# Gated delta rule: the next group's preparation placed step by step in the scan, the last state update left out, and block transfers on two queues

## The reference, cut to what matters

```python
decay = jnp.exp(jnp.where(lower, gc[..., :, None] - gc[..., None, :], -jnp.inf))
a = jnp.where(strict, jnp.einsum('bhncd,bhnsd->bhncs', kb, kc) * decay, 0.0)
t_inv = lax.linalg.triangular_solve(eye + a, jnp.broadcast_to(eye, a.shape),
                                    left_side=True, lower=True, unit_diagonal=True)
...
qk = jnp.einsum('bhncd,bhnsd->bhncs', qc, kc) * decay
...
def step(s, xs):
    qk_i, qd_i, kd_i, u_i, w_i, gl_i = xs
    v_new = u_i - jnp.einsum('bhcd,bhde->bhce', w_i, s)
    o = jnp.einsum('bhcd,bhde->bhce', qd_i, s) + jnp.einsum('bhcs,bhse->bhce', qk_i, v_new)
    s = s * gl_i[..., None, None] + jnp.einsum('bhcd,bhce->bhde', kd_i, v_new)
    return s, o
```

## Time and profile before

| | us |
|---|---|
| median of 3 runs | 3377.32 (3372.14 to 3378.64) |
| the profiled execution | 3375.33 |
| its span, first to last instruction | 3373.5 |
| delta rule's eight groups in it, from 110 to 1325 | 1215 |
| mean granted clock of TensorE | 0.959 |

### The profile page before, as it was taken

One profiled execution on the slowest core, in us unless ns is written; L12 is line 12 of the kernel. 1 busy time (PEld: TensorE's weight loads), 2 busy tenths in 40 slices (PEclk: granted clock), 3 DMA queues, 4 the chain that ended last, 5 costly groups with the idle time before them and its releaser, 6 DMA issues.

```text
span 3373.5 us, 38197 instructions
## 1 busy us (share of the span) xinstructions
PE 3011.8 (89%) x15910; PEld 1901.6 (56%) x15910; DVE 1332.4 (39%) x2862; ACT 980.5 (29%) x2457; POOL 64.5 (2%) x52
## 2 busy tenths in 40 slices
PE   7798988989898876998999889999988989799998
PEld 3476757667676754653655334455454433388743
DVE  3356465555646443622223123322234210377601
ACT  1335435353543523002233122221223310222101
POOL 0000000000000000000000000000000000000000
PEclk9799999999999987998999999999999989899999
DMA  4101101011110104511100012021211012122111
GB/s 195 39 16 45 45 20 39 19 43 32 35 44 20 65 19 176 220 37 45 50 25 19 27 45 82 31 74 51 79 59 75 0 75 100 38 88 83 69 69 42
DMA packets 76509, 196.79 MB, mean 58 GB/s; under 512 B 56144, under 2 KB 61008, under 8 KB 64944
## 3 DMA queue, kind: packets, MB, share of 16 engines
q1 hardware_dynamic: 70064, 173.73, 14.2%
q10 hardware_dynamic: 6272, 20.61, 1.6%
HBM read 182.79 MB, written 11.53 MB: 58 GB/s over the span
## 4 chain that ended last, share of the span: by engine, by line
PE 78%; DVE 9%; ACT 8%; DMA 3%; issue 1%; SPq 1%; DVEq 0%; ACTq 0%
PE ps L935 12%; PE ps L1615 8%; PE ps L1028 5%; PE ps L1552 5%; PE ps L1430 5%; PE ps L1247 3%; PE ps L991 3%; ACT arena L1653 3%; PE ps L1562 2%; PE ps L1434 2%; PE ps L1314 2%; PE ps L925 2%; PE ps L1329 2%; PE ps L1248 2%; ACT arena L1652 2%; PE ps L992 1%
## 5 line engine op out<-in xcount | busy, mean ns | idle before, releaser
L1652 ACT ACTIVATE arena<-ps 64x64 f32<-64x64 f32 (+8 forms) x952 | 314.6, 359 | 1032.8 <-PE ps L935 357.4
L935 PE MATMUL ps<-arena 128*128 128x512 f32 (+1 forms) x976 | 423.5, 593 | 46.1 <-DVE arena L2228 15.2
L935 PEld LDWEIGHTS ps<-arena 128*128 128x128 f32 x976 | 189.3, 195 | 274.5 <-issue 230.4
L991 PE MATMUL ps<-arena 128*128 128x512 f32 x512 | 267.3, 604 | 1.7 <-DVE arena L2228 1.7
L1615 PE MATMUL ps<-arena 128*128 128x256 f32 x1176 | 254.5, 378 | 0.0
L1615 PEld LDWEIGHTS ps<-arena 128*128 128x128 f32 x1176 | 222.2, 189 | 32.6 <-issue 0.5
L1653 ACT ACTIVATE arena<-ps,arena 128x128 f32<-128x128 f32 x544 | 158.4, 369 | 137.7 <-PE ps L1053 50.7
L1552 PE MATMUL ps<-arena 128*128 128x512 f32 x384 | 173.2, 603 | 20.5 <-issue 20.5
L1430 PE MATMUL ps<-arena 128*128 128x512 f32 x384 | 179.8, 596 | 5.2 <-ACT arena L1984 3.5
L1028 PE MATMUL ps<-arena 128*128 128x256 f32 x768 | 180.3, 388 | 0.0
L992 PEld LDWEIGHTS ps<-arena 128*128 128x128 f32 x512 | 98.1, 192 | 126.2 <-issue 126.2
(11 more groups left out here) (295 smaller groups left out, 4193.2 us busy)
## 6 DMA issues: line engine op xcount, KB each, us to landing
arena<-in_ada_w SPq DMA_DIRECT2D x12, 2048.0 KB, 16.9
arena<-in_w_up SPq DMA_DIRECT2D x11, 2048.0 KB, 7.8
arena<-in_w_dil SPq DMA_DIRECT2D x9, 2048.0 KB, 7.7
arena<-in_w_dn SPq DMA_DIRECT2D x8, 2048.0 KB, 10.3
arena<-in_w_gate SPq DMA_DIRECT2D x6, 2048.0 KB, 12.2
arena<-in_w_down SPq DMA_DIRECT2D x8, 1408.0 KB, 5.9
arena<-in_att_in SPq DMA_DIRECT2D x5, 2048.0 KB, 7.7
arena<-in_w_z SPq DMA_DIRECT2D x8, 1024.0 KB, 5.0
```

The lines of the kernel that those rows point to most:

```text
L935: m = e.matmul(out, w[:, (k * m_tiles + x) * 128:(k * m_tiles + x) * 128 + 128], src(k), start=k == 0, stop=k == nk - 1)
L991: e.matmul(ps[:, b1, :], w, uT[:, k * T_ALL + 256:(k + 1) * T_ALL], start=k == 0, stop=k == 7)
L1652: return e.activation(out, x, ACT.Copy)
```

## The change

Five edits, made in all groups but where said. (a) `gram` is taken apart: ScalarE's exponential becomes the step `exp`, and VectorE's three products become `qk`, `at` and `pt`. Inside the scan these are placed one by one: for chunks 0, 1 and 3, whose products fall in steps 3, 4 and 5, `qk` stands behind `scan_s`, `at` behind `scan_v` and `pt` behind `scan_u`. The exponentials of chunks 0 and 1 stand inside step 2, those of 3 and 4 behind step 4, around `decay` 2 and `gram` 3. `decay` 4 moves from behind step 4 to behind step 3. (b) Behind step 5 stand `decay` 5, the exponentials 2 and 5, the first quarter of the following projection `p[0]`, and then `gram` 2 and 5; the products of 4, 2 and 5 come in the order `qk`, `at`, with all three `pt` at the end. Before, `p[0]` followed all of these. (c) `scan_u` and VectorE's part of `scan_v` are left out in step 5, whose state no later step reads; ScalarE's copy there waits for the product itself. (d) For j > 0, four of the eight `blocks_out` transfers of chunks 2 to 5 are issued by ScalarE, ahead of its square `osq`, and for all j four of the eight `back` transfers, behind its turning copy in `solved`. (e) In the start stage ScalarE's copy of the first projection comes ahead of `zg`'s silu, the convolution taps go behind solve steps 5, 8, 10, 12 and 14 (before 3, 5, 8, 10 and 12), and `finish` goes behind solve step 14 (before 12).

```diff
@@ -271,6 +271,9 @@
     def norms(j, n):
         return [("norm_sq", j, n), ("norm", j, n), ("norm_x", j, n), ("turn", j, n)]
 
+    def scaled(j, *chunks):
+        return [(what, j, c) for c in chunks for what in ("qk", "at")] + [("pt", j, c) for c in chunks]
+
     p = project(0)
     yield from p[:6]
     yield from conv(0, 0)
@@ -295,7 +298,9 @@
         yield "spread", 0, c
         yield "decay", 0, c
         yield next(z)
+        yield "exp", 0, c
         yield "gram", 0, c
+        yield from scaled(0, c)
         if c < 2:
             yield next(z)
     for j in range(8):
@@ -321,20 +326,19 @@
         yield "blocks", j
         if j:
             yield "sum_sq", j - 1
-        yield from p[:3]
+        yield from p[1 if j else 0:4]
         if j:
             yield "zg", j - 1
-        yield p[3]
         early = {3: 4, 5: 5, 8: 6, 10: 7, 12: 8, 14: 9}
         for i in range(1, 16):
             yield "solve", j, i
             if i in early:
                 yield p[early[i]]
-                if j < 7 and i < 14:
-                    yield "conv", k, 0, early[i] - 4
+                if j < 7 and i > 3:
+                    yield "conv", k, 0, early[i] - 5
             if i == 8 and j:
                 yield "gate_o", j - 1
-            if i == 12 and j:
+            if i == 14 and j:
                 yield "finish", j - 1
         yield "solved", j
         yield p[10]
@@ -349,26 +353,47 @@
             for c in (0, 1, 2, 4, 3, 5) if (what, size) == ("y", 64) else range(6):
                 yield what, size, j, c
             yield from more
-        also = {s: [] for s in range(6)}
+
+        within, after, scale = ([[] for _ in range(6)] for _ in range(3))
         if j < 7:
-            for s, c in enumerate((0, 3, 4, 2, 5)):
-                also[s].append(("spread", k, c))
-            also[0] += [("spread", k, 1), ("kn", k)]
-            for s, slices in {1: "d0 d1", 2: "g0 d3", 3: "g1", 4: "d4 d2 g3", 5: "g4 d5 g2 g5"}.items():
-                also[s] += [({"d": "decay", "g": "gram"}[x[0]], k, int(x[1])) for x in slices.split()]
+            within = [[("spread", k, 0)], [("spread", k, 3)], [("spread", k, 4), ("exp", k, 0), ("exp", k, 1)],
+                      [("spread", k, 2)], [("spread", k, 5)], [("gram", k, 4)]]
+            after = [[("spread", k, 1), ("kn", k)], [("decay", k, 0), ("decay", k, 1)],
+                     [("gram", k, 0), ("decay", k, 3)], [("gram", k, 1), ("decay", k, 4)],
+                     [("exp", k, 3), ("decay", k, 2), ("gram", k, 3), ("exp", k, 4)], []]
+            scale[3:] = scaled(k, 0), scaled(k, 1), scaled(k, 3)
         else:
-            also[0] += [("mod_turn", 4), ("mod_turn", 5)]
+            after[0] = [("mod_turn", 4), ("mod_turn", 5)]
         for s in range(6):
             yield "scan_s", j, s, 0
             yield "scan_s", j, s, 1
+            yield from scale[s][:1]
             yield "scan_v", j, s, 0
             yield "scan_v", j, s, 1
-            yield from also[s][:1]
-            yield "scan_u", j, s, 0
-            yield "scan_u", j, s, 1
+            yield from scale[s][1:2]
+            yield from within[s]
+
+            if s < 5:
+                yield "scan_u", j, s, 0
+                yield "scan_u", j, s, 1
+            yield from scale[s][2:]
             yield "scan_o", j, s
-            yield from also[s][1:]
-        yield "sum_o", j
+            yield from after[s]
+        if j < 7:
+            yield "decay", k, 5
+            yield "exp", k, 2
+            yield "exp", k, 5
+            yield from scaled(k, 4)[:2]
+            yield "sum_o", j
+            yield project(k + 1)[0] if k < 7 else ("mod_k", 4, 0)
+            yield "gram", k, 2
+            yield "gram", k, 5
+            yield from scaled(k, 2, 5)[:4]
+            yield from (("pt", k, c) for c in (4, 2, 5))
+            yield "blocks_out", k
...
+        def block_out(e, j, first, last, q):
+
+            return e.dma_start(D["blocks"][0, j, q, 2 * first:2 * last].rearrange("c d (k i) -> k (c d) i", k=16),
+                               AT[q * 16:q * 16 + 16, first * 512:last * 512].rearrange(
+                                   "k (u i) -> k u i", i=128)[:, :, q * 16:q * 16 + 16])
+
+        def back(e, j, q):
+
+            return e.dma_start(Yf[q * 16:q * 16 + 16].rearrange("k (u i) -> k u i", u=24)[:, :, q * 16:q * 16 + 16],
+                               D["blocks"][1, j, q].rearrange("c d (k i) -> k (c d) i", k=16))
...
-            def blocks_out(j, part, first, last):
-                for c in range(first, last):
-                    e.wait_ge(*at("inv_dve", j, c, "AT"))
-                for q in range(8):
-                    e.dma_start(D["blocks"][0, j, q, 2 * first:2 * last].rearrange("c d (k i) -> k (c d) i", k=16),
-                                AT[q * 16:q * 16 + 16, first * 512:last * 512].rearrange(
-                                    "k (u i) -> k u i", i=128)[:, :, q * 16:q * 16 + 16]).then_inc(
-                        *landed("blocks_out", j, part, q))
              def blocks_in(j):
-                e.wait_ge(*at("blocks_out", j, 1, 7))
+                e.wait_ge(*at("blocks_out", j, 1, 6 if j else 7))
+                if j:
+                    e.wait_ge(*at("blocks_side", j, 7))
...
-                e.wait_ge(*at("inverses_out", j, 1))
-                e.wait_ge(*at("clean", j))
-                for q in range(8):
-                    e.dma_start(Yf[q * 16:q * 16 + 16].rearrange("k (u i) -> k u i", u=24)[:, :, q * 16:q * 16 + 16],
-                                D["blocks"][1, j, q].rearrange("c d (k i) -> k (c d) i", k=16)).then_inc(
-                        *landed("back", j, q))
...
-                    blocks_out(which[0], 0, 0, 2)
+                    for c in range(2):
+                        e.wait_ge(*at("inv_dve", which[0], c, "AT"))
+                    for q in range(8):
+                        block_out(e, which[0], 0, 2, q).then_inc(*landed("blocks_out", which[0], 0, q))
                 elif what == "blocks":
-                    blocks_out(which[0], 1, 2, 6)
+                    for c in range(2, 6):
+                        e.wait_ge(*at("inv_dve", which[0], c, "AT"))
+                    for q in range(0, 8, 2 if which[0] else 1):
+                        block_out(e, which[0], 2, 6, q).then_inc(*landed("blocks_out", which[0], 1, q))
                     blocks_in(*which)
                 elif what == "solved":
                     inverses_out(*which)
+                    e.wait_ge(*at("inverses_out", which[0], 1))
+                    e.wait_ge(*at("clean", which[0]))
+                    for q in range(0, 8, 2):
+                        back(e, which[0], q).then_inc(*landed("back", which[0], q))
...
-                    e.wait_ge(*at("back", j, 7))
+                    e.wait_ge(*at("back", j, 6))
+                    e.wait_ge(*at("back_side", j, 7))
...
-            def gram(j, c):
+            def exp(j, c):
                 e.wait_ge(*at("inv_pe", j, c, "E"))
                 if j:
                     e.wait_ge(*at("scan_o_pe", j - 1, LEFT[c]))
                 e.activation(PT[:, c * 512:c * 512 + 512], ps[:, GRAM[c], :], ACT.Exp).then_inc(*mark("inv_act", j, c, "E"))
+
+            def gram(j, c):
                 e.wait_ge(*at("inv_pe", j, c, "KK"))
                 for h in range(2):
...
-                e.wait_ge(*at("scan_vd", j, s, d))
+                e.wait_ge(*at("scan_vd", j, s, d) if s < 5 else at("scan_yr", j, s, d))
...
+                elif what == "blocks_out":
+                    j = which[0]
+                    for c in range(2, 6):
+                        e.wait_ge(*at("inv_dve", j, c, "AT"))
+                    for q in range(1, 8, 2):
+                        block_out(e, j, 2, 6, q).then_inc(*landed("blocks_side", j, q))
...
                     solved(*which)
+                    j = which[0]
+                    e.wait_ge(*at("inverses_out", j, 1))
+                    e.wait_ge(*at("clean", j))
+                    for q in range(1, 8, 2):
+                        back(e, j, q).then_inc(*landed("back_side", j, q))
...
-            def gram(j, c):
-                a, o = AT[:, c * 512:c * 512 + 512], PT[:, c * 512:c * 512 + 512]
-                lane, before = {0: (0, None), 1: (1, None), 3: (2, None), 4: (0, 0), 2: (1, 1), 5: (2, 3)}[c] if j else (
-                    c % 3, c - 3 if c > 2 else None)
-                qk = rsA[:, 256 * lane:256 * lane + 256].rearrange("p (d s) -> p d s", d=2)
+            def qk_of(c):
+
+                lane = {0: 0, 1: 1, 3: 2, 4: 0, 2: 1, 5: 2}[c]
+                return rsA[:, 256 * lane:256 * lane + 256].rearrange("p (d s) -> p d s", d=2)
+
+            def qk(j, c):
+                before = {4: 0, 2: 1, 5: 3}.get(c)
                 e.wait_ge(*at("inv_act", j, c, "KB"))
                 if before is not None:
                     e.wait_ge(*at("inv_dve", j, before, "PT"))
```

(15 more changed lines are left out.)

19 lines of the change are left out of this document (14 added, 5 removed).

## The result

| | before | after |
|---|---|---|
| median | 3376.02 us (3372.14 to 3378.64, 4 runs) | 3265.85 us (3263.36 to 3267.29, 4 runs) |
| the profiled execution's span | 3373.5 us | 3261.5 us |
| mean granted clock of TensorE | 0.959 | 0.967 |

The ratio is 0.9674, with a 95% interval of 0.9657 to 0.9691: 110 us less. The forecast was 3273: 3258 to 3286 by itself, and as far as the first rival's 3301 as a whole.

The account below looks back on a forecast made before the run. TensorE, busy 89% of the span, loses time where it stands still. Savings of 72.9 (scans), 18.8 (groups 1 to 6), 12.3 (group 7) and 0.5 (last scan) sum to 104.5 us: median 3273, range 3258 to 3286, chance 0.70.

Parts of the forecast that it names:

- the first rival: Block transfers: two queues work one after the other, so splitting issues saves nothing; 28 us dearer, 3301; chance 0.12.
- Scans (forecast 37.0 us each): Each scan falls from 47.13 us to 37.0 as most TensorE stalls go; scans 0 to 5 gain 72.9 together.
- S: Mark in the timeline: the start of a scan.
- rival 2: Scan steps 3, 4 and 5: VectorE's products still hold the scan up, one 0.9 us stall each; 3292; chance 0.12.
- Exponential 0's 0.71: In the scan, TensorE's 0.71 us stall for this exponential stays, as it remains behind four spread copies on ScalarE.
- The new wait ahead of the last `scan_o`: End of the scan: late ScalarE copies of `scan_v` 5 add a wait of 0.6 us, possibly 0 to 1.2.
- The unread update: Scan step 5: leaving out L1169's state update saves 1.07 us by the spacing of starts.
- From the projection to J: Projection's start to first join J: comes at 41.0 us, 0.7 of it TensorE waiting; groups 1 to 6 gain 18.8.
- GpSimd's hold: Start stage: GpSimd's 3.44 us product slows VectorE's work beside it; 3.3 us added to the solve chain.
- Group 7 (forecast −12.3: After scan 6: last AT comes 8.5 us earlier and the split saves 1.9 twice, 12.3 us less.
- The last scan (forecast −0.5: Final scan, without `scan_u` and with ScalarE released one operation earlier: 0.5 us less.
- Rivals 3 and 4: ScalarE's block issues make it slower, 3385, chance 0.02; or waits restore the old order, nothing changes, 3377, chance 0.02.

## Why the prediction was right

**Scans (forecast 37.0 us each).** Right, 0.55 too long. From S to the old place of the projection it is 36.45. The residual stalls are gone, and their return costs 4 to 5.6 us per scan (products together), so they were caused by the three products in a row, and rival 2 is out. Exponential 0's 0.71 stayed, and its cause was the spread copies. The new wait ahead of the last `scan_o` is smaller than 0.6: by the starts it is 0.27 (L1215 comes 0.49 after L1086, whose two records take 0.22 elsewhere), and the products of `scan_o` take 0.17 longer than in step 4 (1.06 against 0.89 to the next line's start), 0.44 together. But the update was worth 0.2 less than forecast (next paragraph), so these two cancel, and the 0.55 lies in a term that the sum doesn't have: behind a stall the next spacing is longer too. In scan 6 before the change, next to the earlier trace rows:

```profile
1154.99 0.39 PE L1053 MATMUL ps<-arena 128*128 128x128 f32 x2
...
1160.15 1.22 PE L1169 MATMUL ps<-arena 128*128 128x256 f32 x4
```

L1053 comes 0.32 us after the L1052 that had stalled, and 0.22 where nothing stalls (L1085 and L1086 above); L1169 comes 1.23 after the stalled L1160, and 1.13 in the earlier trace rows. So a stall that went was worth about 0.25 more than its row says and not 0.16, and six went: with the 0.09 that the sum lacks for each, 0.5 to 0.6 us. Moving the exponentials ahead of the spread copies shows the same, 0.98 us for a stall of 0.71. Full clock in all seven was forecast, and came.

**The unread update.** The sum took 1.07 us for it, less 0.6 for a new wait, 0.47 in all. Measured it is 0.87 less 0.44: with the update kept in the otherwise changed kernel the scan is 0.42 longer. Both terms were too large, and the difference is right.

**From the projection to J (forecast 41.0 us with 0.7 of waiting for TensorE).** Two terms missed in opposite directions. Counted from the projection's old place (S + 36.45, 948.97 in group 6; the expectations above count it 0.1 later, and so have 41.35 for J):

| | forecast | group 6 |
|---|---|---|
| the blocks' first issue of the split | 5.6 | 5.63 |
| solve starts | 11.6 | 11.70 |
| solve to inverses out | 23.0 | 22.49 |
| inverses out to J | 6.4 | 7.26 |
| J | 41.0 | 41.45 |
| TensorE's wait in it | 0.7 | 1.27 |

The chain of VectorE is 0.5 shorter: GpSimd's hold is 2.87 us and not the 3.3 that I took for it. The transfers back are 0.9 longer, and this is the term that was mis-sized: I took half the issues to be worth half the time, 1.9. With eight on one queue J comes 5.91 us after the first issue (473.07 − 467.16, in the kernel with one queue), with four on each 4.88 (990.42 − 985.54). The issues end 1.96 earlier, yet what follows the last issue grows from 2.03 to 2.95. Running only these on one queue costs 1.1 per group in S to J, which says the same. The wait for the blocks is for this reason 1.3 to 1.8 us and not under 1, as "What would show it" had it. Outward the half was right: from the first issue to L833 it is 3.48 us in group 7 (1085.13 to 1088.61) against 5.27 before. Rival 1, that the queues work one after the other, is out: the issues of both lie beside each other, and without the second queue the kernel takes 3302.

The Trainium skill, "DMA: Bandwidth & Descriptors", "Issuing engines are not separate DMA queues", says that a second issuer saves only the issue time, which is usually small. The saving here is no more than the issue time, as it says; but for transfers as small as these the issue time is the larger part.

Over groups 1 to 6 the six scans take 218.7 us where 222 was forecast, and the stretches to J 249.6 where it was 246. The two errors have nothing to do with each other and cancel, so S of scan 0 to S of scan 6 came out at −91.6 against −91.7. That is luck.

**GpSimd.** The prediction had "a VectorE operation of some 3 us in every start"; it is the tap, 3.88. "SBUF — State Buffer", "SBUF: two separate sides", of the Trainium skill has an exclusive lock on the shared port. The runs agree: with the product cut, the same tap takes 1.01.

**Group 7 (forecast −12.3, measured −11.2).** The blocks' first issue comes 41.10 us after S of scan 6 instead of 49.51, −8.4 where 8.5 was forecast; outward the split gives 1.8 of 1.9 and back 1.0 of 1.9. That last is nearly the whole miss.

**The last scan (forecast −0.5, measured −2.3).** From step 2 on it is 29.00 against 29.64 us, −0.6. The rest is the first two steps, which run at a granted clock of 0.83 instead of 0.66, behind a start of 5.06 us of waiting that is the same in both kernels:

```profile
1170.08:1180.08 10.00, 10.00 (x56) 8.63 (x57) 5.75 (x17) 5.19 (x18) 0.33 (x1) 0.83 0.49 210
```

In the seven experiments that leave the last scan and VectorE's part of the gate behind it as they are, it takes 39.0 to 40.3 for the same instructions. So the clock alone moves it by 1.3 us from run to run, and I don't count the 1.7 as an effect of the change.

**Not in the working:** 2.7 us ahead of scan 0 and 4.3 behind the last transposes. The code there is the same but for the split `gram` of group 0. S of scan 0 lies at 252.7 to 256.3 in the experiments, which share that part, and what follows the last transposes takes 2050.4 to 2055.9 in them, so both are of about the size of their own spread. Without both, the measured sum is 105.0 (91.62 + 11.22 − 0.15 + 2.29) against the forecast's 104.5.

**Rivals 3 and 4** are out: ScalarE's issues take 0.47 to 0.48 us each in all groups of the profile, and the stalls that were to go went.

**What stays open.** Why ScalarE's four issues take 3.57, 3.07 or 3.54 us in one group each of three kernels. It is not the order of the exponentials: it is seen in the kernel with the update kept too (3.07), and in the changed kernel's two profiles never. There SyncE's four beside them took 3.03, while in the other two kernels SyncE's took the usual 1.79. No experiment was made on it.

## What to carry to other kernels

Where several in-order engines work on a loop, put the side work between the steps at the place where its engine waits anyway, one operation at a time: three operations of 0.4 to 0.7 us in a row ahead of a critical one, three times a scan, cost 4 us per scan here. When a stretch has two chains of nearly the same length, first find the later one: feeding TensorE earlier (`p[0]`) cost 8 us while VectorE's chain was last, and changed the time by less than could be measured once it wasn't. And price a stall of TensorE with the clock that it leaves behind, which in one kernel here added half as much again.

## What the runs showed of the hardware

**The clock behind a wait.** A stretch from the first join to the scan takes 53.6 us at full clock. Behind waits of up to 1.9 us it did so in groups 1 to 6 of every kernel profiled. Behind 4.2 to 4.6 us it took 55.0 to 56.3. Between them it went either way: 1.97 us (products together) was followed by 55.16 and 2.37 by 55.15, but 2.38 and 2.70 (update kept) by 53.6. A wait of 3.01 (exponentials first) was followed by 56.32.

**Transfers back over two queues land later.** Four issues on each of two queues end 1.96 us sooner than eight on one, and the data are there only 1.0 sooner. For the transfers out it is 1.8 of 1.9.

**ScalarE's issues vary.** Four of the outward ones take 1.86 to 1.88 us nearly everywhere, but 3.57, 3.54 and 3.07 in single groups.

**GpSimd's memset didn't hold VectorE's product.** GpSimd's product makes VectorE's tap nearly four times as long, or, when VectorE is ahead, takes 5.49 instead of 3.49 us itself; PT beside its memset takes what it takes alone, 0.69:

```profile
1077.14 2.66 POOL L2872 MEMSET arena<- 128x3072 f32 x1 [109.01 <-PE ps L1194]
...
1077.28 0.69 DVE L2373 TENSOR_TENSOR arena<-arena 128x512 f32<-128x512 f32 x1
```
